# Alternating the two token tiles from matmul to matmul in a decoder block with split-precision weights

## The reference

```python
h = layer_norm(DN_ALPHA * h + 0.5 * swiglu(h, ffn1_wg, ffn1_wu, ffn1_wd), ln1_g, ln1_b)
mix = token_mixer(h, w_in, ...)   # attention with 16 heads and a conformer convolution, gated and projected
h = layer_norm(DN_ALPHA * h + mix, ln2_g, ln2_b)
h = layer_norm(DN_ALPHA * h + 0.5 * swiglu(h, ffn2_wg, ffn2_wu, ffn2_wd), ln3_g, ln3_b)
# swiglu(x, wg, wu, wd) = (silu(x @ wg) * (x @ wu)) @ wd, with wg and wu 2048 x 5632 and wd 5632 x 2048
```

## Time and profile before

| | |
|---|---|
| median of the runs | 2275.11 us |
| span of the profiled execution | 2273.0 us |
| PE busy | 2250.2 us (99%), 10160 matmuls |
| PEld busy | 1866.7 us (82%) |
| DVE busy | 1252.9 us (55%) |
| ACT busy | 976.1 us (43%) |
| DMA queue of the loads | 56.2% of the 16 engines' time, 191 GB/s |

### The profile page before, as it was taken

The page is one execution under the profiler, slowest core; times in us unless marked ns, Lnnn a source line. Parts: engine busy times, 40 slices in busy tenths (PEclk is TensorE's granted clock), DMA queues, the critical chain, the costliest instruction groups (busy, mean ns, idle before and its releaser), DMA issues.

```text
span 2273.0 us, 29283 instructions
## 1 busy us (share of the span) xinstructions
PE 2250.2 (99%) x10160; PEld 1866.7 (82%) x10160; DVE 1252.9 (55%) x1392; ACT 976.1 (43%) x1087; POOL 5.1 (0%) x13
## 2 busy tenths in 40 slices
PE   8999999999999999999999999999999999999997
PEld 7888888888888888888888888888888888888886
DVE  5545444454445747777776365667444454544544
ACT  5444444433333544554545443434444444433431
POOL 0000000000000000000000000000000000000000
PEclk9999999999999999999999999999999999999999
DMA  8656555555556564545455565646565555555554
GB/s 297 203 170 215 175 197 177 192 200 173 192 191 241 175 202 160 193 165 184 159 176 196 196 203 170 238 159 206 174 211 179 190 185 184 197 191 200 188 187 146
DMA packets 118993, 434.16 MB, mean 191 GB/s; under 512 B 13344, under 2 KB 13728, under 8 KB 118048
## 3 DMA queue, kind: packets, MB, share of 16 engines
q1 hardware_dynamic: 118944, 433.52, 56.2%
HBM read 431.37 MB, written 2.10 MB: 191 GB/s over the span
## 4 chain that ended last, share of the span: by engine, by line
PE 98%; DVE 1%; DMA 0%; POOL 0%; issue 0%; SPq 0%; ACT 0%; DVEq 0%; POOLq 0%
PE acc L916 32%; PE acc L914 32%; PE acc L915 32%; PE tb L962 2%; DVE act_sb L614 0%; PE tb L1055 0%; PE tb L1069 0%; DMA raw<-in_stream 0%; DVE res L620 0%; PE tb L1054 0%; PE tb L1070 0%; DVE stats L598 0%; DVE res L592 0%; POOL rstd L905 0%; DVE mv L603 0%
## 5 line engine op out<-in xcount | busy, mean ns | idle before, releaser
L569 DVE TENSOR_TENSOR w_lo<-raw,w_hi 128x1024 fp32r<-128x1024 f32 x800 | 960.7, 1222 | 680.3 <-ACT w_hi L355 664.8
L355 ACT ACTIVATE w_hi<-raw 128x1024 fp32r<-128x1024 f32 x800 | 831.9, 1059 | 680.5 <-PE acc L916 555.4
L914 PE MATMUL acc<-w_hi,xT_hi 128*128 128x512 f32 x2176 | 853.6, 392 | 7.6 <-DVE w_lo L569 7.6
L916 PE MATMUL acc<-w_hi,xT_lo 128*128 128x512 f32 x2176 | 848.0, 390 | 0.0
L915 PE MATMUL acc<-w_lo,xT_hi 128*128 128x512 f32 x2176 | 847.5, 389 | 0.0
L914 PEld LDWEIGHTS acc<-w_hi,xT_hi 128*128 128x128 f32 x2176 | 409.0, 188 | 91.9 <-DVE w_lo L569 8.7
L916 PEld LDWEIGHTS acc<-w_hi,xT_lo 128*128 128x128 f32 x2176 | 408.9, 188 | 85.5
L915 PEld LDWEIGHTS acc<-w_lo,xT_hi 128*128 128x128 f32 x2176 | 409.3, 188 | 83.3
L914 PE MATMUL acc<-w_hi,hT_hi 128*128 128x512 f32 x704 | 274.2, 389 | 0.0
L916 PE MATMUL acc<-w_hi,hT_lo 128*128 128x512 f32 x704 | 273.9, 389 | 0.0
L915 PE MATMUL acc<-w_lo,hT_hi 128*128 128x512 f32 x704 | 273.9, 389 | 0.0
(11 more groups left out here) (88 smaller groups left out, 667.9 us busy)
## 6 DMA issues: line engine op xcount, KB each, us to landing
raw<-in_stream SPq DMA_DIRECT2D x800, 512.0 KB, 4.5
ln_gb<-in_ln SPq DMA_DIRECT2D x6, 1024.0 KB, 7.8
res<-in_x_rows SPq DMA_DIRECT2D x1, 2048.0 KB, 9.8
out<-res SPq DMA_DIRECT2D x8, 256.0 KB, 2.7
x_stage<-in_xT SPq DMA_DIRECT2D x3, 512.0 KB, 6.8
cgb<-in_conv_ln SPq DMA_DIRECT2D x2, 512.0 KB, 4.3
x_stage<-in_xT SPq DMA_DIRECT2D x2, 256.0 KB, 4.0
alibi<-in_consts SPq DMA_DIRECT2D x1, 200.0 KB, 5.5
```

What stands on the lines that cost most here:

```text
L355: act.activation(w_hi[:, seg.split(j)], raw[:, seg.raw(j)], ACT.Copy).then_inc(hi_ready, 1)
L569: dve.tensor_tensor(w_lo[:, s], raw[:, seg.raw(j)], f32(w_hi[:, s]), ALU.subtract).then_inc(lo_ready, 1)
L914: pe.matmul(out_ap, x[0][:, k, rows], w_hi[:, s, cols], start=begin, stop=False)
L916: return pe.matmul(out_ap, x[1][:, k, rows], w_hi[:, s, cols], start=False, stop=end)
```

## The change

Chunks without hooks no longer go through their groups tile by tile. A new function, `both_tiles`, takes each of the three parts of a block for tile 0 and then at once for tile 1, so that the stationary operand and the PSUM bank change with every matmul, and the moving operand with every second one. The waits for both banks stand ahead of the chunk's first matmul. `tile0_full` is raised by the chunk's last matmul but one.

```diff
+            def both_tiles(seg, i, j0, n, pair, x, use, units):
+
+                if units[0] == 0:
+                    for t in range(TT):
+                        v = 2 * use + (t - 1)
+                        if not (isinstance(v, int) and v <= 0):
+                            pe.wait_ge(acc_out[pair], v)
+                for j in units:
+                    pe.wait_ge(lo_ready, seg.unit(i, j0 + j) + 1)
+                    s = seg.split(j0 + j)
+                    for b in range(UK):
+                        k, cols = UK * j + b, slice(b * COLS, (b + 1) * COLS)
+                        begin, end = j == 0 and b == 0, j == n - 1 and b == UK - 1
+                        tiles = [(t, acc[:, 2 * pair + t], slice(t * P, (t + 1) * P)) for t in range(TT)]
+                        for t, out_ap, rows in tiles:
+                            pe.matmul(out_ap, x[0][:, k, rows], w_hi[:, s, cols], start=begin, stop=False)
+                        for t, out_ap, rows in tiles:
+                            pe.matmul(out_ap, x[0][:, k, rows], w_lo[:, s, cols], start=False, stop=False)
+                        for t, out_ap, rows in tiles:
+                            mm = pe.matmul(out_ap, x[1][:, k, rows], w_hi[:, s, cols], start=False, stop=end)
+                            if t == 1 and b == UK - 1:
+                                mm.then_inc(unit_used, 1)
+                            elif t == 0 and end:
+                                mm.then_inc(tile0_full, 1)
+
             def chunk(seg, i, j0, n, pair, x, use, groups=None, after={}, ready={}):
...
                 for units in groups or groups_of(n):
+                    if not after and not ready:
+                        both_tiles(seg, i, j0, n, pair, x, use, units)
+                        continue
                     for t in range(TT):
```

## The result

| | before | after | forecast |
|---|---|---|---|
| median of the runs | 2275.11 us | 2345.05 us (2344.64 to 2346.57) | 2338.3 (2321 to 2349) |
| ratio | | 1.031 (1.0295 to 1.032) | 1.028 |
| span of the profiled execution | 2273.0 us | 2344.7 us | 2336.2 |

The account below looks back on a forecast made before the run. PE, busy 99%, was taken as the bound: 9600 matmuls 0.227 us apart. Distance 0, pauses 46.1, end 5.1 and clock 12 gave 63.2 us, span 2273.0 to 2336.2, median 2338.3 us; 8-in-10 range 2321 to 2349.

Parts of the forecast that it names:

- the pauses: New PE waits at 14 chunk starts in `down`, `mix_out`, `gates` and `attn_out`, 46.1 us in all.
- the clock: Each of six pauses in `down` brings PE's clock down, 2.0 us each, 12 us; bounds 0 and 22.
- The distance between matmuls: In the 5136 alternating matmuls, changing banks gains 0; bounds 69 us gained, 5 us lost.
- The other-pair chunks: Where the next chunk uses the other bank pair, as in `up`, the new waits cost nothing.
- the way back from the taker to PE: At each chunk start that waits, 0.05 us from the taking instruction's end to PE, an estimate.
- DVE's steps: In each `down` pause: first add 0.60, three units 3.40, `bn_stats` 0.60, second add 0.67 us.
- The end: Behind the last matmul, tile 0's rows no longer run beside PE: 5.1 us more.
- The row of the start: At the kernel's start matmuls run at half clock for some 5 us, losing 2.5 us.
- A: Rival: the waits come as forecast but the clock stays up, 2326.3 us; 15%.
- B: Rival: the clock falls in `mix_out` and perhaps `gates` too, 2.5 us in nine places, 2348 us; 12%.
- C: Rival: changing banks frees PE of 0.0135 us in all 5136 matmuls, 2269 us; 6% with its variants.
- D: Rival: takers find their banks sooner, so the change does almost nothing, 2275 to 2280 us; 1%.

Follow-up runs that it names:

- the fillers: The changed kernel with four rows of 16 unused matmuls at the three chunk starts of the first `down`; timed once, 2356.65 us.
- the filler experiment: The changed kernel with 20 unused matmuls ahead of the wait at each of the six chunk starts of `down`; 2331.19 us.
- the first experiment: The changed kernel with alternation kept only where no bank is awaited soon (3840 matmuls); 2275.29 us, ratio 1.000.
- the experiments with pauses: The changed kernel with three units' `w_lo` behind both adds (2318.22 us), 20 unused matmuls per `down` start (2331.19 us), or four rows of 16 (2356.65 us).

## Why the prediction was right, step by step

The mechanism came as forecast in all four parts. Two sizes were too small, the pauses (by 0.2 us each) and the clock (16.9 us against 12), so the measured 2345.05 us lies at the upper edge of the 2330 to 2345 that the forecast gave itself.

**The distance between matmuls** was put at 0 gained. Right: 1.000 with 3840 alternating matmuls, and equal distances in the fillers. The single bank change in the earlier trace rows had told it, though it was thin evidence for a steady alternation. The Trainium skill's 215.7 ns (TensorE: Matmul & The Clock Gate, "Wait — 56ns, not 53.3ns?") isn't reached by any version here; these float32 matmuls pay 13 ns beyond their columns and not 2.5.

**The pauses** came in all 14 places and nowhere else. The other-pair chunks cost nothing. Their size was short by 0.2 us each: 2.8 of 46 us. The term that was off is the way back from the taker to PE, which I put at 0.05 without a row. In `down` the second add ends at 564.42 + 0.67 = 565.09 and PE starts at 565.33: 0.24. The 14 places have 0.24 to 0.27. DVE's steps themselves were right: 559.80 to 565.09 is 5.29, against 5.27 counted.

**The end** was right: 5.1 us, alone and in the sum.

**The clock** did fall in each of the six pauses of `down`, and the filler experiment shows that the idle time is the cause. The size was 16.9 us against 12. The row of the start had given 2.5 a fall, and I went below it to 2.0 for no reason that a row gave. The six falls of `down` cost 2.0 to 2.8 each, 2.5 in the mean (31 us of work at half pace, and slower restarts), and a seventh came in `mix_out` for 1.6, which I had kept in the range only. The Trainium skill's rule in the same page, that idleness takes the clock down and sustained work brings it back, agrees in its direction: in the pause shown above the clock fell 2.7 us in, and was back after 4.1 us of work.

**The rivals.** A (clock stays up) is excluded by the stretches at 0.50. B was partly true: one fall more than the six, where it has three. C (banks give back 0.0135) and D (no waits) are excluded by the first experiment and by the waits.

## What to carry to other kernels

A bank of sums that two neighbouring chunks share is free only as long as it is full early. Reordering within a chunk that makes both tiles complete together puts everything that the other engines do between their two takings into TensorE's wait, even when no instruction is added. So read, for each bank, how long before its next use it is complete, and what stands on the taking engine in between. On an engine that is busy 99%, a pause costs its length and, if it is long, the clock as well: here all pauses of 5.5 us brought it down, half of those of 2.3 us, and none of 1.5 us or less. Where a wait of some microseconds can't be avoided, unused matmuls in it can pay: here they gave back 14 of 70 us.

## What was unexpected of the hardware

The same length of pause sometimes brings the clock down and sometimes not. Over four kernels (the changed one and the experiments with pauses), all pauses of 5.5 us without fillers did (nine of nine), those of 2.3 us did in 9 of 18, and none of 1.5 us or less. What decides between them isn't shown. Of the nine falls behind a pause of 2.3 us, eight came after PE had resumed, by 0.1 to 1.4 us (1.4 in the rows of `mix_out` above), and each left 0.50 for 3.4 us and cost 1.5 to 1.7 us. Behind the pauses of 5.5 us the clock always fell within the pause, stood at 0.50 for 6.8 us, and cost 2.0 to 2.8 us.

A float32 matmul here has a fixed price of 0.013 us above its columns at 2.4 GHz (0.227 for 512, 0.120 for 256), and one of 128 columns takes 0.11 us, which that price doesn't explain. At half clock the price doesn't show: 0.427 is 512 / 1.2.

In the 14 pauses of the changed kernel PE starts 0.24 to 0.27 us after the end of the instruction that it waited for, while DVE and ACT start 0.13 to 0.17 us after the modelled end of the matmul that they waited for. Behind the kernel's last matmul DVE needs only 0.03 to 0.04 us for this (from 2259.33 + 0.39 = 2259.72 to 2259.75).
